# A banded attention stage: the third turned group's copy between the two exponents, turned behind the second score chunk, and the mask added by products of 128 columns

## What is computed

```python
# blocks of 128 queries; each sees three blocks of latent keys (before, own, after) and 256 context keys
valid = ((jnp.abs(qpos[:, :, None] - kpos[:, None, :]) <= WINDOW)      # WINDOW = 128
         & (kpos[:, None, :] >= 0) & (kpos[:, None, :] < S))
s_band = jnp.einsum('bnqhgd,bnkhd->bnhgqk', qb, kband) * SWA_SCALE
s_band = jnp.where(valid[None, :, None, None], s_band, NEG_INF)
s_ctx = jnp.einsum('bnqhgd,bkhd->bnhgqk', qb, k_ctx) * SWA_SCALE
p = softmax([s_band, s_ctx, s_sink])
out = einsum(p_band, vband) + einsum(p_ctx, v_ctx)
```

## Time and profile before

| | |
|---|---|
| median of 3 timed runs | 1397.72 us |
| profiled execution | 1399.78 us |
| its span | 1398.0 us |
| mean granted TensorE clock | 0.988 |
| TensorE products, busy | 1357.5 us, 97% |
| VectorE, busy | 914.6 us, 65% |
| ScalarE, busy | 692.6 us, 50% |
| POOL, busy | 487.1 us, 35% |
| the band in the span | from about 231 to 360 us |
| mask products L1372 | 88: 64 of 128 columns, 24 of 384 |

### The profile page before, as it was taken

One profiled execution on the slowest core, in us unless ns is written; L12 is line 12 of the kernel. 1 busy time (PEld: TensorE's weight loads), 2 busy tenths in 40 slices (PEclk: granted clock), 3 DMA queues, 4 the chain that ended last, 5 costly groups with the idle time before them and its releaser, 6 DMA issues.

```text
span 1398.0 us, 18825 instructions
## 1 busy us (share of the span) xinstructions
PE 1357.5 (97%) x7262; PEld 1149.4 (82%) x7262; DVE 914.6 (65%) x1284; ACT 692.6 (50%) x1343; POOL 487.1 (35%) x321
## 2 busy tenths in 40 slices
PE   5899997999999999999999999999999999999999
PEld 1688987999899988988887888888888888888887
DVE  1878776777777877875774646547564654746463
ACT  2755655788778777972223424333332433333240
POOL 2766553121299992501102303132050323205010
PEclk8999998999999999999999999999999999999999
DMA  9555658433365646301123112121211212121013
GB/s 377 192 162 160 177 159 286 129 89 86 115 199 144 190 131 191 71 1 61 31 76 121 31 31 90 31 75 31 62 44 30 91 31 75 30 62 44 15 61 121
DMA packets 121576, 143.42 MB, mean 103 GB/s; under 512 B 8184, under 2 KB 103288, under 8 KB 118672
## 3 DMA queue, kind: packets, MB, share of 16 engines
q1 hardware_dynamic: 121232, 142.18, 32.6%
q0 software_dynamic: 256, 0.05, 0.0%
HBM read 108.38 MB, written 31.74 MB: 100 GB/s over the span
## 4 chain that ended last, share of the span: by engine, by line
PE 70%; DVE 11%; POOL 7%; ACT 6%; DMA 4%; issue 1%; SPq 1%; DVEq 0%; ACTq 0%; POOLq 0%
PE f_ps L2062 24%; PE f_ps L2331 19%; PE o_ps L1770 6%; PE a_ps L1422 4%; PE a_ps L1438 3%; PE f_ps L2347 3%; POOL l_wg L1349 3%; ACT s_pr L1519 3%; POOL l_gate L1351 3%; PE t_ps L956 2%; PE a_ps L1468 2%; DVE s_nmx L1604 2%; PE t_ps L945 1%; DMA t_wm<-in_w_mod 1%; DMA l_v<-scratch_v 1%
## 5 line engine op out<-in xcount | busy, mean ns | idle before, releaser
L2062 PE MATMUL f_ps<-h,f_w 128*128 128x512 f32 x1536 | 358.0, 389 | 0.4 <-DVE h L1836 0.2
L2062 PEld LDWEIGHTS f_ps<-h,f_w 128*128 128x128 f32 x1536 | 288.1, 188 | 60.7 <-DVE h L1836 0.7
L2261 DVE TENSOR_TENSOR mix<-mix,f_ps 128x512 f32<-128x512 f32 x196 | 128.7, 683 | 152.9 <-PE f_ps L2331 152.9
L2102 POOL TENSOR_TENSOR f_w<-f_w,f_g 128x1024 f32<-128x1024 f32 x30 | 77.0, 2590 | 390.2 <-DMA f_w<-in_w_mlp 342.7
L2139 ACT ACTIVATE f_a<-f_ps 128x512 f32<-128x512 f32 x64 | 38.2, 597 | 254.7 <-PE f_ps L2062 254.7
L2331 PE MATMUL f_ps<-f_bh,f_al 128*128 128x512 f32 x392 | 152.5, 389 | 0.0
L2331 PE MATMUL f_ps<-f_bh,f_ah 128*128 128x512 f32 x392 | 152.5, 389 | 0.0
L2331 PE MATMUL f_ps<-f_bl,f_ah 128*128 128x512 f32 x392 | 152.5, 389 | 0.0
L1618 DVE TENSOR_TENSOR l_pT<-a_ps,l_pT 128x512 fp32r<-128x512 f32 (+1 forms) x192 | 108.9, 594 | 54.0 <-ACT l_pT L1529 53.9
L1422 PE MATMUL a_ps<-l_k,l_q 96*128 96x512 f32 (+1 forms) x576 | 136.5, 366 | 1.6 <-DMA l_v<-scratch_v 1.1
L956 PE MATMUL t_ps<-w_in,t_h 128*128 128x416 f32 (+2 forms) x600 | 125.7, 355 | 0.3 <-DVE w_in L719 0.3
(11 more groups left out here) (223 smaller groups left out, 2425.1 us busy)
## 6 DMA issues: line engine op xcount, KB each, us to landing
l_wg<-in_w_mod SPq DMA_DIRECT2D x8, 2048.0 KB, 8.0
f_w1r<-in_w_mlp SPq DMA_DIRECT2D x32, 512.0 KB, 4.0
f_w<-in_w_mlp SPq DMA_DIRECT2D x16, 1024.0 KB, 5.0
t_wm<-in_w_mod SPq DMA_DIRECT2D x8, 1024.0 KB, 12.5
scratch_k<-t_kT SPq DMA_DIRECT2D x20, 384.0 KB, 3.7
l_k<-scratch_k SPq DMA_DIRECT2D x8, 960.0 KB, 10.6
scratch_q<-t_qT SPq DMA_DIRECT2D x16, 384.0 KB, 3.9
l_q<-scratch_q SPq DMA_DIRECT2D x8, 768.0 KB, 6.3
```

The source lines that it names most:

```text
L2062: last = nc.tensor.matmul(ps[:, b, :], w1[:, g % 2, w, k, :], h2[x][:, k, half * HB:(half + 1) * HB], start=(k == 0 and i == 0), stop=(k = ...
L2261: V.tensor_tensor(x, x, ps[:, bank_of(i, t), :].rearrange("p (k c) -> p k c", c=P), ALU.add).then_inc(added, 1)
```

## The change

Three edits.

1. `score`: the mask is added by one product of 128 columns for each outer key block of the chunk, none for the middle one. A chunk of three key blocks has two mask products of 128 columns in place of one of 384; all other chunks keep theirs.
2. `band_scores`: the third group of step `s - 2` is turned behind the second chunk, in both parities. In narrow steps that is where it stood.
3. `scalar`: `third_hi(s - 1)` stands between the two exponents of the band, no longer behind them.

```diff
         if cut:
-            d0, d1 = (0, 1) if first == 0 and n < 3 else (2 - first, 3 - first) if first and n < 3 else (0, 3)
-            ins = MM(fps[:, a + d0 * P:a + d1 * P], identr[:, :], edger[:, (first + d0) * P:(first + d1) * P],
-                     start=False, stop=True)
+            outer = [d for d in range(n) if first + d != 1]
+            for d in outer:
+                ins = MM(fps[:, a + d * P:a + d * P + P], identr[:, :], edger[:, (first + d) * P:(first + d) * P + P],
+                         start=False, stop=(d == outer[-1]))
         return ins
@@ band_scores
         for i, (hh, c) in enumerate(todo):
-            if i and hh != todo[i - 1][0] and s >= 2:
+            if i == 2 and s >= 2:
                 third(s - 2)
@@ scalar
             if 1 <= s < W:
                 band_exp(s, 1 - s % 2, shared_read)
+                third_hi(s - 1)
                 band_exp(s, s % 2, exped)
-                third_hi(s - 1)
                 if s % 2 == 0 and s >= 4:
                     low((s - 4) // 2)
```

## The result

The changed kernel took 1406.09 us, the median of four runs between 1405.65 and 1406.77; the kernel before took 1398.65, now the median of four runs as well. The ratio is 1.0054 with a 95% interval of 1.0039 to 1.0069: slower by 7.4 us. The forecast was slower by 5.6 us, 1403.3, with a range up to 1405.7; the time lies 0.4 us above that range. The profiled execution took 1406.77 us, with a span of 1404.9 against 1398.0.

The account below looks back on a forecast made before the run. A 4.02 us ScalarE-VectorE loop was taken to bound the band; a new TensorE-ScalarE loop of 4.23 replaces it. The groups' +2.82 and +2.76, together +5.6, on 1397.72 give 1403.3 us; range 1399.5 to 1405.7.

Parts of the forecast that it names:

- What bounded before, and what the change frees: In the band, a ScalarE-VectorE loop of 4.02 us a step bounds; moving the copy drops it to 3.25, TensorE's 3.87 next.
- The new loop: Band: third turning, copy, second exponent, next turning, values, scores: 4.24 us a step, 4.23 with odd steps, 0.21 longer than before.
- the copy's hold on ScalarE: Third group's copy keeps ScalarE 0.26 us before the second exponent in each band step.
- The waits: TensorE stands still 0.37 us every band step before the next turning; VectorE's 0.8 us wait on the copy goes.
- The masks: Band mask products go from 88 to 112; at most +1.0 us, at best -1.4, taken as 0 because hidden.
- the upper bound: Two 128-column mask products instead of one of 384 cost at most 0.04 us more, times 24: +1.0 us.
- If that wait is not there, they count: Mask products cost time if TensorE's 0.37 us wait before the band's next turning is absent; at most +1.0 us.
- Group ends: Last step of each 12-step group carries about 0.6 us of the loss; second group's first third turning is held, +0.22.
- From the sum to the time: Band's shift passes through the later chain unchanged; median 1397.72, 2.06 below the profiled execution, plus 5.6 gives 1403.3 us.
- The rivals: For the whole kernel: faster, 1394.1 us, 8%; no difference, middle 1399, 12%; slower still, 1405.7, 12%.
- In time: Third turned group reaches ScalarE by the first exponent's end; TensorE's 3.87 us bounds: -3.6 us, 1394.1; chance 8%.

Follow-up runs that it names:

- the last run of the experiments: Kernel before with the third group's copy on VectorE, the fifth head's loads ahead of the gate row's, and 128-column masks: 1395.14 us against 1399.44, ratio 0.9970.

## Why the prediction was right in kind and short in size

- *What bounded before, and what the change frees.* Right. TensorE's lines are in the chain now, VectorE's maximum is not.
- *The new loop.* The right links, and their sum short by 0.05 us a step. The links in the trace of the changed kernel: scores to third turning 0.71 (266.85 to 267.56; predicted 0.70), to the copy 0.48 (0.48), to the second exponent 0.28 (0.26), its time 0.88 (0.87), to TensorE's load 0.05 (0.06), turning 0.83 (0.83), values 1.05 (1.04): 4.28 us. In even steps the largest error is the copy's hold on ScalarE: its price came from a copy followed by an eviction; followed by an exponent it holds 0.02 us more. In odd steps it is the turning. Its two loads are further apart, 0.24 us together instead of 0.20, and from the first load (271.81) to the copy (272.33) it takes 0.52 us, not 0.48:

```profile
271.12 0.41 PEld L1369 LDWEIGHTS a_ps<-s_k,s_q 128*128 128x128 f32 x2
...
271.81 0.24 PEld L1439 LDWEIGHTS a_ps<-ident,s_pr 128*128 128x128 f32 x2
```
```profile
272.33 0.38 ACT L1530 ACTIVATE s_pT<-a_ps 128x256 fp32r<-128x256 f32 x1 [0.29 <-PE a_ps L1439]
```

  I had taken the odd steps as 0.02 us shorter; they are as long as the even ones. Over the two groups that is 1.1 us too little. The 0.22 us too much at the second group's start (below) takes some of it back, and 0.9 is the whole difference between 5.6 and the 6.5 of the groups.
- *The waits.* TensorE's is 0.31 us in the row, 0.37 worked out; the split masks' 0.04 have taken part of it. VectorE's wait for the copy did not go away, though I had written that it does: 0.64 of its 0.80 us are still there, since the copy itself now waits for the turned group, and 0.30 stand ahead of the maximum.
- *The masks.* Right, in size and in being hidden. From the mask's load to the second load of the scores behind it were 0.35 us (267.65 to 267.83 + 0.36 - 0.19), and are 0.39 now (268.36 to 268.64 + 0.30 - 0.19): the 0.04 of the upper bound. They lie in front of TensorE's wait, and 24 of them cost nothing measurable, in the changed kernel or alone. "If that wait is not there, they count" came true too, in the last run of the experiments.
- *Group ends.* Right at the end: the last step of each group is 0.6 us longer. Wrong at the second group's start: a hold of 0.22 us was added to its first step, but that step lasts 4.05 us (313.64 to 317.69), as the first group's does (4.04). The sums are 50.77 against 50.22 predicted and 50.80 against 50.44.
- *From the sum to the time.* This is the step that failed. I took 2.06 us off the profiled 1399.78 to come to the base, 1397.72, a median of three runs, and gave it no uncertainty. That base was low, by chance as far as the record shows. A fourth run makes it 1398.65, and in the 70 runs beside the experiments the medians are 1399.78, 1399.73 and 1399.44, level with the profiled execution: 0 to 0.3 us should have come off, not 2.06. The second term that was too small is the loop's, by 0.9 us. With either alone the time would have stayed in the range: 1397.72 + 6.5 = 1404.2, and 1399.4 to 1399.8 + 5.6 = 1405.0 to 1405.4. With both right the sum is 1405.9 to 1406.3; measured were 1406.09 and 1405.96.
  Where single executions differ is shown in part. The two executions of the changed kernel that have a trace differ by 1.8 us in their spans (1404.9 and 1403.1), and 1.5 of it is there before the first group starts, at 249.15 in the one and at 247.63 in the other; why, stays open. I had also found nothing behind the band that hangs on an earlier clock. The wait for a head's loads may be such a thing, 1.4 us before and 1.9 and 2.0 in those two executions. Whether that half microsecond belongs to the change stays open too: other kernels whose loads stand behind the same gate row show 0 to 1.9.

```profile
247.63 0.77 PEld L1464 LDWEIGHTS a_ps<-s_pT,s_v 128*128 128x128 f32 x4
```
- *The rivals.* "In time" failed for the reason given: the path is longer than its cover. With the cover lengthened by 0.44 us (the first exponent's head turned first) TensorE's own work did bound, though at 3.98 and not 3.87 us.

## What to carry to other kernels

When an instruction is moved ahead in an engine's queue because someone waits for it, follow what it waits for itself: everything behind it inherits that wait, and if the producer in turn waits for one of those, a new loop is closed whose length is the sum of its links. Work out that sum before the gain. If the moved work can go to an engine with idle time instead, as the copy went to VectorE here, both loops can be gone. A forecast of a time needs the spread of the base as well as that of the change: a base from three runs was some 2 us off here, where the change was worth 6.5.

## What the runs showed of the hardware

- A VectorE instruction of two columns with both operands in SBUF, which takes 0.16 us elsewhere, took 0.59 while POOL worked on two SBUF tensors, and ended with POOL's instruction (270.39 and 270.40). In the run with the first exponent's head turned first, in POOL's timeline and in VectorE's:

```profile
268.86 1.53 POOL L1336 TENSOR_TENSOR mix<-s_both,s_crossed 64x256 f32<-64x256 f32 x2 [6.89 <-DMA s_crossed<-s_both]
```
```profile
269.81 0.59 DVE L1614 TENSOR_TENSOR s_shift<-s_nmx,nsink 128x2 f32<-128x2 f32 x1
```

  The exponent behind it started 0.4 us late, and the wide step there lasted 4.45 us (268.85 to 273.30) between neighbours of 3.95. The Trainium skill, "SBUF — State Buffer", section "SBUF: two separate sides", says that VectorE and GpSimd (POOL in the rows) share a pair of ports, and that of a VectorE instruction with two inputs in SBUF and a GpSimd instruction that reads SBUF, whichever starts first holds it for its whole length; the rows agree. In the changed kernel it took 0.40, from 270.71, and POOL's ended at 271.09.
- After a wait for a head's loads the granted clock was lower in one execution. In the run with the turning alone, TensorE waited 1.9 us for them, and behind it the granted clock of the stretch from 490 to 500 us was 0.83, a part of it at the lower of the two levels (1.2 of 2.4 GHz); in the kernel before, after a wait of 1.4 us, it was 1.00 in the same stretch. TensorE was 0.2 us behind the kernel before where this head starts, and 1.7 where the next one does. The length of the wait alone doesn't decide it: the changed kernel waited 1.9 us as well, and its clock was 1.00 behind it.

```profile
490.00:500.00 10.00, 8.97 (x52) 8.30 (x53) 5.34 (x8) 5.37 (x13) 10.00 (x2) 0.83 0.55 211
```
```profile
495.00:500.00 5.00, 3.29 (x22) 2.77 (x21) 2.60 (x4) 2.73 (x7) 5.00 (x2) 1.00 0.34 79
500.00:505.00 5.00, 5.00 (x40) 4.68 (x39) 4.02 (x6) 3.75 (x9) 5.00 (x1) 1.00 0.99 364
```
  The first row is the turning alone, the other two the changed kernel. The columns are TensorE's products, its weight loads, VectorE, ScalarE and POOL, busy us and instructions each, the granted clock, the share of the DMA engines and GB/s.
